# A hybrid attention and expert layer on one core: expert gates written by accumulating indirect DMA instead of one-hot matrix products

## The chip, the cores and the metric

The kernel runs on one core of one Trainium2 chip, written directly against the engines (each engine has its own instruction list and waits on counting semaphores). The metric is device microseconds of that core, lower is better.

## The reference

One decoder layer over 16 meta tokens and 256 sequence tokens, width 2048, float32. Two attention branches and a gated merge come first; the change lies in the last part, the expert mixer:

```python
def peer(h, w_query, sub_keys, expert_u, expert_v):
    ...
    s = jnp.einsum('thcd,hcnd->thcn', q, sub_keys).astype(jnp.float32)
    v1, i1 = lax.top_k(s[:, :, 0], PEER_TOPK)
    v2, i2 = lax.top_k(s[:, :, 1], PEER_TOPK)
    cand = (v1[..., :, None] + v2[..., None, :]).reshape(n_tok, PEER_HEADS, PEER_TOPK * PEER_TOPK)
    best, j = lax.top_k(cand, PEER_TOPK)
    e_idx = (jnp.take_along_axis(i1, j // PEER_TOPK, axis=-1) * PEER_N_KEYS
             + jnp.take_along_axis(i2, j % PEER_TOPK, axis=-1))
    gate = jax.nn.softmax(best, axis=-1)
    ...
        a = jax.nn.gelu(jnp.einsum('cd,chkd->chk', tc, u_sel).astype(jnp.float32), approximate=False)
        w = (gc * a).astype(tc.dtype)
        return jnp.einsum('chk,chkd->cd', w, expert_v[ec])
```

There are 8 heads, each picks 16 of 128 x 128 = 16384 experts for each of the 256 tokens. The kernel computes it densely: gelu(token x every u row), times a gate that is zero except for the picks (summed over heads), times every v row.

## The kernel before, in words

All weights, 376 blocks of 1 MB, pass once through the core in one stream of 752 halves of 512 KB (`load`, L361). The blocks are, in order: 80 for the attention heads (`F_BRANCH` = 80), 16 for the branch outputs, 16 for the output projection, 8 for the query, 128 for u (from block `F_U` = 120), 128 for v (from block `F_V` = 248). The matrices are multiplied as float32 split in two reduced parts, so each half passes three engines:

- SP loads half k into one of four buffers `raw` when the half four places ahead in the stream has been split (`lo_done`).
- ACT copies it to its high part `whi` (`hi_half`, L342), four halves ahead of PE.
- DVE subtracts, `wlo` = `raw` - `whi` (`lo_half`, L349), two halves ahead of PE; `wlo` has two buffers.
- PE multiplies. In `mul_half` (L402, L403, L407) a half takes 24 matmuls of 256 tokens; in `value_block` (L634, L640) it takes 12 of 512 columns.

Each engine's other work is written by hand into slots between the halves.

**u, first 64 blocks** (halves 0 to 127 of the stage). Scores against the sub-keys (L569) are made first. ACT copies them for the first 128 tokens (L817), DVE for the other 128 (L1126), and PE waits for ACT's copy alone before its first u block. ACT then writes gelu of each finished block into `W` (L831). DVE picks: one turn for each of 16 (token tile, head) pairs, spread over the slots of 8 halves (L1143 to L1180).

**Between the two halves of u.** DVE normalises all gates (L1186 to L1190), PE transposes the picked indices and gates (L605), and DVE splits the gates into three bf16 parts (L1197 to L1201).

**u, last 64 blocks.** Beside the stream the dense gates are made, two tokens for each half: DVE builds one-hot rows (`make_rows`, L1213 to L1215), ACT scales two of them (`scale_rows`, L845), PE multiplies them (`gate_pair`, L588, six small matmuls a half) into PSUM, and DVE multiplies the gates of four tokens into `W` over all experts (`apply_gates`, L1234). `W` of these blocks must hold something before, so POOL fills it with ones and gelu comes in by a product (`apply_gelu`, L1240).

```python
            for t in range(2):
                out_ = bank(2 + u // 2 % 2, (2 * (u % 2) + t) * P, P)
                for n in range(3):
                    last = mm(out_, hots[:, u % 2, t, 0, :], hots[:, u % 2, t, 1 + n, :],
                              start=n == 0, stop=n == 2)
```

**v.** `W` of each block is split in a high part (`weight_hi`, L868, ACT) and a low part (`weight_lo`, L1264, DVE), and PE multiplies them by the v rows into all eight PSUM banks. The last token group of the gates has to be applied (L1234) before the first of these.

The buffer `arena` holds `W` (128 x 32768 float32). Its blocks 96 and up also hold what the picks need until they have been used. POOL's only DMAs before are 16 small ones that rearrange rows for the attention (L891).

Of the kernel before, what the change touches and what calls it, by code (L numbers as in the profile page):

```python
# [33 lines left out]
P = 128  # L34
# [27 lines left out]
F_G = F_U + B_U // 2  # L62
# [9 lines left out]
          ("mean128", P), ("swap", P), ("ident", P), ("iota", P), ("iota16", TOPK), ("one", 1), ("rows01", 3)]  # L72
# [13 lines left out]
def shape_constants():  # L86
# [31 lines left out]
    put("iota", np.arange(P)[None, :])  # L118
# [41 lines left out]
def hybrid_layer(nc, stream, x_t, params, consts, h1_rows, out):  # L160
    with ExitStack() as ctx:
# [98 lines left out]
        st = r_work.again().take(4 * HEADS * NK).rearrange("p (i c n) -> p i c n", i=2 * HEADS, c=2)  # L260
# [3 lines left out]
        chosen_i = w4.take(2 * 2 * NSEL).rearrange("p (c s) -> p c s", c=2)  # L264
        chosen_g = w4.take(2 * NSEL)
        gate_sum = w4.take(4 * HEADS)
# [10 lines left out]
        best_all = small[:, 1024:1024 + 2 * NSEL]  # L277
        eq = w4.take(2 * TOPK * TOPK).rearrange("p (c k m) -> p c k m", c=2, k=TOPK)

        part = [small[:, n * P:(n + 1) * P].bitcast(BF16) for n in range(3)]  # L280
        left = [small[:, 512 + n * T:512 + (n + 1) * T] for n in range(2)]

        hots = small[:, 0:1024].bitcast(BF16).rearrange("p (b t n i) -> p b t n i", b=2, t=2, n=4)
        iota_bf = small[:, 1024:1024 + P // 2].bitcast(BF16)
        row2 = small[:, 1088:1088 + 2 * P].bitcast(BF16).rearrange("p (b t i) -> p b t i", b=2, t=2)

        idx_ps = [psum[:, 5 * 512 + n * T:5 * 512 + (n + 1) * T] for n in range(4)]
        gate_sb = [xr[:, 2 * KC * T + n * T:2 * KC * T + (n + 1) * T] for n in range(2)]
# [5 lines left out]
        Whi = [xr[:, n * 2 * T:n * 2 * T + T] for n in range(2)]  # L294
        Wlo = [xr[:, n * 2 * T + T:(n + 1) * 2 * T] for n in range(2)]
# [4 lines left out]
        def f(ap):  # L300
# [23 lines left out]
        sc_ready, sc_taken, best_sub, best_exp, chosen, choice_ps = (  # L324
            sem("head_scores_ready"), sem("head_scores_taken"), sem("best_less_max"), sem("best_exp"), sem("chosen"),
            sem("choice_transposed"))
        const_used, ones_early, ones_late = sem("constants_used"), sem("early_ones_set"), sem("late_ones_set")
        o_ms, o_std_done, heads_normed = sem("head_out_mean_square"), sem("head_out_std"), sem("head_out_normed")
        row_ready, gate_split = sem("one_hot_rows"), sem("gate_parts")
        first_weights = sem("first_weights_done")  # L330
        hot, gate_ps, gated, gelu_done = sem("one_hots"), sem("gates_psum"), sem("gates_applied"), sem("gelu_done")
# [22 lines left out]
        def _(sp):  # L354
# [16 lines left out]
            with sp.Fori(0, BLOCKS // 2 - 1) as i:  # L371
# [18 lines left out]
        def _(pe):  # L390
# [182 lines left out]
            pe.wait_ge(scores_sb, 1)  # L573


            with pe.Fori(0, B_U // 4) as i:
                for q in range(2):
                    mul_block(i * 4 + 2 * F_U, 2 * q, i * 2 + (F_U + q + 1), bank(q, 0, T), hi, lo)


            def gate_pair(i, u):
                pe.wait_ge(hot, i * 4 + (u + 1))
                if u % 2 == 0:
                    pe.wait_ge(gated, i * 2 + (u // 2 + 1))
                for t in range(2):
                    out_ = bank(2 + u // 2 % 2, (2 * (u % 2) + t) * P, P)
                    for n in range(3):
                        last = mm(out_, hots[:, u % 2, t, 0, :], hots[:, u % 2, t, 1 + n, :],  # L588
                                  start=n == 0, stop=n == 2)
                last.then_inc(gate_ps, 1)  # L590

            def late_half(i, m):

                c, j = m // 2, m % 2
                if j == 0:
                    pe.wait_ge(bank_free, i * 2 + (F_G + c + 1))
                mul_half(i * 4 + 2 * F_G, m, bank(c % 2, 0, T), hi[8 * j:8 * j + 8], lo[8 * j:8 * j + 8],
                         j == 0, j == 1)

            late_half(0, 0)  # L600

            pe.wait_ge(chosen, 1)
            for n, src in enumerate((chosen_i[:, 0, :], chosen_i[:, 1, :], chosen_g)):
                for b in range(2):
                    last = nc.tensor.transpose(idx_ps[n][:, b * P:(b + 1) * P], src[:, b * P:(b + 1) * P], C["ident"])  # L605
            last.then_inc(choice_ps, 1)

            late_half(0, 1)
            late_half(0, 2)
            gate_pair(0, 0)  # L610
            late_half(0, 3)
            gate_pair(0, 1)
            gate_pair(0, 2)
            with pe.Fori(0, B_U // 4 - 1) as i:
                for m in range(4, 8):
                    late_half(i, m)
                    gate_pair(i, m - 1)
            gate_pair(0, T // 2 - 1)


            def value_block(base, c, w_base, first):
                pe.wait_ge(w_hi, w_base + c + 1)
                for j in range(2):
# [3 lines left out]
                    if first and j:  # L627
                        pe.wait_ge(gated, T // 4 + 2)
# [16 lines left out]
            pe.wait_ge(bank_free, 2 + F_V)  # L645
# [8 lines left out]
        def _(act):  # L654
# [161 lines left out]
            for c in range(2):  # L816
                last = A(st[:, 0:HEADS, c, :], bank(SCORES[0][c], 0, HEADS * NK).rearrange("p (h n) -> p h n", h=HEADS),  # L817
                         ACT.Copy)
# [4 lines left out]

            act.wait_ge(scores_sb, 1)
            act.wait_ge(scores_dve, 1)
            with act.Fori(0, 2 * HEADS) as i:
                act.wait_ge(sc_taken, i + 1)
                A(sc, st[:, ds(i, 1), :, :].rearrange("p a c n -> p (a c) n"), ACT.Copy).then_inc(sc_ready, 1)
                for q in range(4):
                    act.wait_ge(half_done, i * 8 + (2 * F_U + 2 * q + 2))  # L830
                    A(one_weight(i * 4 + q), bank(q % 2, 0, T), ACT.Gelu).then_inc(bank_free, 1)  # L831
                    for j in range(2):
                        hi_half(act, i * 8 + 2 * F_U, 2 * q + 4 + j)
            A(gate_sum[:, 0:1], C["eps"], ACT.Exp)
            act.wait_ge(best_sub, 1)
            A(chosen_g, chosen_g, ACT.Exp).then_inc(best_exp, 1)


            act.wait_ge(gate_split, 1)

            def scale_rows(i, u):
                act.wait_ge(row_ready, i * 4 + (u + 1))
                for t in range(2):
                    for n in range(2):
                        last = A(hots[:, u % 2, t, 1 + n, :], row2[:, u % 2, t, :], ACT.Copy,  # L845
                                 scale=f(gate_sb[n][:, ds(i * 8 + (2 * u + t), 1)]))
                last.then_inc(hot, 1)

            def act_late_slot(i, m):
                act.wait_ge(half_done, i * 4 + (2 * F_G + m + 1))  # L850
                if m % 2:
                    A(bank(m // 2 % 2, 0, T), bank(m // 2 % 2, 0, T), ACT.Gelu).then_inc(gelu_done, 1)
                hi_half(act, i * 4 + 2 * F_G, m + 4)

            scale_rows(0, 0)
            act_late_slot(0, 0)
            scale_rows(0, 1)
            with act.Fori(0, B_U // 4 - 1) as i:
                for m in range(1, 5):
                    act_late_slot(i, m)  # L860
                    scale_rows(i, m + 1)
            for m in range(B_U - 3, B_U):
                act_late_slot(0, m)
                if m < B_U - 1:
                    scale_rows(0, m + 1)

            def weight_hi(chunk, q):
                A(Whi[q], one_weight(chunk), ACT.Copy).then_inc(w_hi, 1)  # L868


            act.wait_ge(half_done, 2 * F_V)
            act.wait_ge(first_weights, 1)
            act.wait_ge(bank_free, 2 + F_V)
            for q in range(2):
                weight_hi(q, q)
            with act.Fori(0, B_V // 2 - 1) as i:
                for q in range(2):
                    act.wait_ge(half_done, i * 4 + (2 * F_V + 2 * q + 2))
                    act.wait_ge(gated, T // 4 + 2)
# [6 lines left out]
        def _(pool):  # L886

            pool.wait_ge(cum_done, 1)
# [4 lines left out]
            a = r_work.a  # L893
            pool.wait_ge(rows_ps, 3)
            pool.wait_ge(key_scores, 2)
# [11 lines left out]
        def _(dve):  # L907
# [217 lines left out]
            for c in range(2):  # L1125
                last = V.tensor_copy(st[:, HEADS:2 * HEADS, c, :],  # L1126
                                     bank(SCORES[1][c], 0, HEADS * NK).rearrange("p (h n) -> p h n", h=HEADS))
# [220 lines left out]
```

## Time and profile before

| what | before |
|---|---|
| median of three runs | 2360.9 us (2359.17 to 2360.91) |
| the profiled execution: its span, the only time given for it | 2360.5 us |
| PE busy, share of the span | 2309.6 us, 98% |
| DVE busy | 1566.1 us, 66% |
| ACT busy | 1281.2 us, 54% |
| POOL busy | 22.0 us, 1% |
| DMA read | 400.5 MB |

"PE" is the matmul side of TensorE, "PEld" its weight loads, "DMA share" the mean busy share of the 16 DMA engines, "PEclk" the granted TensorE clock as a share of 2.4 GHz. Since successive matmuls overlap, the duration of one is longer than the step from one to the next; the step is read from the chain of waits, which gives each matmul only the time that it adds. An idle time before an instruction is put down to the one that released it.

### The profile page before, as it was taken

The numbers are of one execution on the slowest core, as the hardware profiler recorded it, in microseconds if no ns is written. First come the engines' busy times: TensorE is split into PE (matmuls) and PEld (weight loads), VectorE is DVE, ScalarE is ACT, GpSimd is POOL, SyncE is SP. The second block draws the span as 40 slices with busy tenths as digits, with TensorE's granted clock in tenths as the row PEclk, the third lists the DMA queues.
The fourth block names the chain that finished last, engine by engine and source line by source line (L and its number), as shares of the span: only waits on it lengthen the run. The fifth ranks groups of instructions, "written<-read, shape, count | busy, mean of one in ns | idle before, by whom it ended". The sixth has DMA issues, their size and how long they took to land.

```text
span 2360.5 us, 48307 instructions
## 1 busy us (share of the span) xinstructions
PE 2309.6 (98%) x16398; PEld 2145.8 (91%) x16398; DVE 1566.1 (66%) x2913; ACT 1281.2 (54%) x2068; POOL 22.0 (1%) x25
## 2 busy tenths in 40 slices
PE   6999999999999899999989999999999999999998
PEld 5999999998999899999989999999788888888887
DVE  6666665566664557777779999999555555555555
ACT  5555555555553445555548888888344444444443
POOL 1000000000000010000010000000000000000000
PEclk9999999999999999999999999999999999999999
DMA  4444444444454445555544444444455555555555
GB/s 178 152 151 157 145 154 157 150 151 151 160 178 169 170 160 185 179 177 187 180 143 157 160 160 160 161 163 161 171 195 190 193 195 191 192 195 192 191 194 204
DMA packets 111701, 405.05 MB, mean 172 GB/s; under 512 B 12864, under 2 KB 12992, under 8 KB 111424
## 3 DMA queue, kind: packets, MB, share of 16 engines
q1 hardware_dynamic: 111024, 402.65, 49.7%
q10 hardware_dynamic: 144, 2.10, 0.2%
q8 instruction: 14, 0.23, 0.0%
q0 software_dynamic: 512, 0.02, 0.0%
q14 instruction: 7, 0.06, 0.0%
HBM read 400.50 MB, written 4.19 MB: 171 GB/s over the span
## 4 chain that ended last, share of the span: by engine, by line
PE 96%; DVE 2%; ACT 0%; DMA 0%; issue 0%; DVEq 0%; SPq 0%; ACTq 0%
PE psum L402 20%; PE psum L407 20%; PE psum L403 20%; PE psum L634 20%; PE psum L640 10%; PE psum L588 2%; PE psum L511 0%; PE psum L510 0%; PE psum L479 0%; PE psum L433 0%; PE psum L470 0%; PE psum L478 0%; DVE xr L1201 0%; PE psum L569 0%; DMA arena<-x_t 0%
## 5 line engine op out<-in xcount | busy, mean ns | idle before, releaser
L349 DVE TENSOR_TENSOR wlo<-raw,whi 128x1024 fp32r<-128x1024 f32 x752 | 918.2, 1224 | 652.9 <-PE psum L640 339.2
L402 PE MATMUL psum<-xr,whi 128*128 128x256 f32 (+1 forms) x3968 | 998.4, 289 | 10.4 <-DVE xr L1056 9.0
L403 PE MATMUL psum<-xr,whi 128*128 128x256 f32 (+1 forms) x3968 | 977.9, 283 | 0.0
L342 ACT ACTIVATE whi<-raw 128x1024 fp32r<-128x1024 f32 x752 | 761.5, 1048 | 79.3 <-PE psum L407 63.6
L402 PEld LDWEIGHTS psum<-xr,whi 128*128 128x128 f32 x3968 | 757.5, 191 | 13.0 <-issue 7.4
L403 PEld LDWEIGHTS psum<-xr,whi 128*128 128x128 f32 x3968 | 758.3, 191 | 1.0
L407 PE MATMUL psum<-xr,wlo 128*128 128x256 f32 (+1 forms) x3968 | 559.7, 284 | 8.4 <-DVE wlo L349 8.4
L407 PEld LDWEIGHTS psum<-xr,wlo 128*128 128x128 f32 x3968 | 514.4, 192 | 8.9 <-DVE wlo L349 8.8
L634 PE MATMUL psum<-whi,xr 128*128 128x512 f32 x2048 | 506.8, 390 | 2.6 <-DVE arena L1240 2.6
L634 PEld LDWEIGHTS psum<-whi,xr 128*128 128x128 f32 x2048 | 384.9, 188 | 82.8 <-DVE arena L1240 2.7
L640 PE MATMUL psum<-wlo,xr 128*128 128x512 f32 x1024 | 274.5, 390 | 0.0
L868 ACT ACTIVATE xr<-arena 128x256 fp32r (+1 forms) x128 | 53.6, 419 | 399.2 <-PE psum L640 397.8
L640 PEld LDWEIGHTS psum<-wlo,xr 128*128 128x128 f32 x1024 | 192.8, 188 | 40.1
L845 ACT ACTIVATE small<-small,xr 128x128 bf16<-128x128 bf16 x512 | 163.5, 390 | 85.6 <-DVE small L1215 85.5
L831 ACT ACTIVATE arena<-psum 128x256 f32 x64 | 24.6, 385 | 146.8 <-PE psum L407 146.6
L1234 DVE TENSOR_TENSOR arena<-arena,psum 128x512 f32 (+1 forms) x63 | 85.2, 1353 | 0.0
L1215 DVE TENSOR_SCALAR small<-small,psum 128x128 bf16<-128x128 bf16 x256 | 81.8, 319 | 0.0
L1213 DVE TENSOR_SCALAR small<-small,psum 128x128 bf16<-128x128 bf16 x256 | 65.0, 254 | 3.1 <-PE psum L588 3.0
L588 PE MATMUL psum<-small 128*128 128x128 bf16 x768 | 65.3, 222 | 0.4 <-ACT small L845 0.4
L697 ACT ACTIVATE arena<-psum 128x256 f32<-128x256 f32 (+1 forms) x32 | 12.6, 393 | 96.5 <-PE psum L407 96.5
L1214 DVE TENSOR_SCALAR small<-small,psum 128x128 bf16<-128x128 bf16 x256 | 65.0, 254 | 0.0
L1264 DVE TENSOR_TENSOR xr<-arena,xr 128x256 fp32r<-128x256 f32 x128 | 53.5, 419 | 0.0
(219 smaller groups left out, 1082.6 us busy)
## 6 DMA issues: line engine op xcount, KB each, us to landing
raw<-stream SPq DMA_DIRECT2D x752, 512.0 KB, 3.2
arena<-x_t SPq DMA_DIRECT2D x4, 544.0 KB, 6.5
h_rows<-arena ACTq DMA_DIRECT2D x1, 2048.0 KB, 11.2
raw<-h_rows SPq DMA_DIRECT2D x4, 512.0 KB, 4.4
out<-arena SPq DMA_DIRECT2D x8, 256.0 KB, 3.1
arena<-consts SPq DMA_DIRECT2D x1, 1066.0 KB, 13.2
arena<-params SPq DMA_DIRECT2D x1, 739.0 KB, 10.4
arena<-arena POOLq DMA_DIRECT2D x16, 1.1 KB, 3.2
```

The lines of the kernel that those rows point to most:

```text
L342: nc.scalar.activation(whi[:, s * HALF:(s + 1) * HALF], raw[:, s * HALF:(s + 1) * HALF], ACT.Copy).then_inc(hi_done, 1)
L349: nc.vector.tensor_tensor(wlo[:, k % 2 * HALF:(k % 2 + 1) * HALF], raw[:, s * HALF:(s + 1) * HALF], f(whi[:, s * HALF:(s + 1) * HALF]), AL ...
L402: mm(acc, w, hi[c], start=start and c == 0, stop=False)
L403: mm(acc, w, lo[c], start=False, stop=False)
L407: last = mm(acc, wlo[:, s * HALF + c * P:s * HALF + (c + 1) * P], hi[c], start=False, stop=stop and c == 7)
L588: last = mm(out_, hots[:, u % 2, t, 0, :], hots[:, u % 2, t, 1 + n, :], start=n == 0, stop=n == 2)
L634: mm(bank(b * 4 + j * 2 + n), part[c % 2][:, b * P:(b + 1) * P], whi[:, s * HALF + n * 512:s * HALF + (n + 1) * 512], start=first and part ...
L640: last = mm(bank(b * 4 + j * 2 + n), Whi[c % 2][:, b * P:(b + 1) * P], wlo[:, s2 * HALF + n * 512:s2 * HALF + (n + 1) * 512], start=False, ...
L845: last = A(hots[:, u % 2, t, 1 + n, :], row2[:, u % 2, t, :], ACT.Copy, scale=f(gate_sb[n][:, ds(i * 8 + (2 * u + t), 1)]))
L1213: V.tensor_scalar(hots[:, u % 2, t, 0, :], iota_bf, i1, None, ALU.is_equal)
L1215: last = V.tensor_scalar(hots[:, u % 2, t, 3, :], iota_bf, i2, gate, ALU.is_equal, ALU.mult)
L1234: V.tensor_tensor(w, w, bank(2 + n % 2).rearrange("p (t c) -> p t c", t=4), ALU.mult).then_inc(gated, 1)
```

## The change

The gates are written to a 16.8 MB tensor `gates_at` [128, 128, 256] in device memory (first key, second key, token) and read back one block at a time.

- POOL fills the tensor with zeros in the attention stage: 8 transfers of 2 MB, cut in rows of 512 bytes, one as each head begins.
- DVE finishes each turn of 16 picks inside the turn: address = expert x 256 + token, softmax over the 16. ACT makes the exponentials (L818 of the new file) in the turn too. The turns alternate between the token tiles.
- POOL issues for each of the 16 turns 16 indirect transfers with `compute_op=ALU.add`, each of 128 single float32 values, 256 in all. It waits for the turn's picks, and for the turn two before to have landed.
- PE's u stage is one loop of 128 plain blocks, without one-hot products or transposes. Its accumulators move to banks 2 and 3, so PE waits at its start for DVE's first copy of scores instead of ACT's.
- ACT waits for all scatters before it writes gelu of block 96; SP waits for them before it loads half 488 (8 halves before the end of the u stage).
- SP loads 128 KB of gates for each v block, two ahead, and DVE multiplies them in (`gate_weights`), before both parts of the weight are split off. POOL's fills with ones are gone.

```diff
 @@ SP
+            EARLY = F_V // 2 - 3
+            with sp.Fori(0, EARLY) as i:
...
+            def load_gates(c, n):
+                sp.dma_start(gate_in[n], gates_at[:, ds(c, 1), :].rearrange("p a t -> p (a t)")).then_inc(gates_in[n], 16)
+
+            for b in range(2):
+                sp.wait_ge(scattered[b], 16 * NSEL)
+            for n in range(2):
+                load_gates(n, n)
+            for k in range(4 * EARLY, 2 * F_V):
+                sp.wait_ge(lo_done, k + 1)
+                load(k + 4, k % 4)
+            with sp.Fori(0, B_V // 2 - 1) as i:
+                for q in range(2):
+                    sp.wait_ge(lo_done, i * 4 + (2 * F_V + 2 * q + 1))
+                    load(i * 4 + (2 * F_V + 2 * q + 4), 2 * q)
+                    sp.wait_ge(scaled, i * 2 + (q + 1))
+                    load_gates(i * 2 + (q + 2), q)
+                    sp.wait_ge(lo_done, i * 4 + (2 * F_V + 2 * q + 2))
+                    load(i * 4 + (2 * F_V + 2 * q + 5), 2 * q + 1)
 @@ PE
-            pe.wait_ge(scores_sb, 1)
-            with pe.Fori(0, B_U // 4) as i:
+            pe.wait_ge(scores_dve, 1)
+            with pe.Fori(0, B_U // 2) as i:
                 for q in range(2):
-                    mul_block(i * 4 + 2 * F_U, 2 * q, i * 2 + (F_U + q + 1), bank(q, 0, T), hi, lo)
-            def gate_pair(i, u):
...
+                    mul_block(i * 4 + 2 * F_U, 2 * q, i * 2 + (F_U + q + 1), bank(2 + q, 0, T), hi, lo)
 @@ ACT
+            act.wait_ge(zeroed, 16 * HEADS)
+            with act.Fori(0, HEADS) as i:
+                for b in range(2):
...
+                        if q == 2:
+                            act.wait_ge(best_ready, i * 2 + (b + 1))
+                            A(gate_exp, best, ACT.Exp, bias=neg_best, accum_out=gate_sum[:, 0:1]).then_inc(best_exp, 1)
...
+            expert_blocks(B_U // 2, 3 * B_U // 4)
+            for b in range(2):
+                act.wait_ge(scattered[b], 16 * NSEL)
+            act.wait_ge(rows_out, 16)
+            expert_blocks(3 * B_U // 4, B_U - 4)
 @@ POOL
+            for h in range(HEADS):
+                pool.wait_ge(o_ready, 2 * h + 1)
+                pool.dma_start(blank[:, h * width:(h + 1) * width].rearrange("p (a n) -> p a n", n=P),
+                               spread(zeros.unsqueeze(1), 1, width // P)).then_inc(zeroed, 16)
+            pool.wait_ge(zeroed, 16 * HEADS)
+            every = gates_at.rearrange("p c t -> (p c t)").unsqueeze(1)
+            for h in range(HEADS):
+                for b in range(2):
+                    pool.wait_ge(picked, 2 * h + b + 1)
+                    if h:
+                        pool.wait_ge(scattered[b], 16 * TOPK * h)
+                    for k in range(TOPK):
+                        at = (2 * h + b) * TOPK + k
+                        pool.indirect_dma_start(every, bass.IndirectOffsetOnAxis(pick_at[:, at:at + 1], 0),
+                                                pick_gate[:, at:at + 1], None, compute_op=ALU.add
+                                                ).then_inc(scattered[b], 16)
 @@ DVE
+                        ch.link(V.scalar_tensor_tensor(expert, chosen[:, 0, :], float(NK), chosen[:, 1, :], ALU.mult, ALU.add))
+                        V.tensor_scalar(pick_at[:, mine], expert, float(T), C["token"][:, b:b + 1], ALU.mult, ALU.add)
+                        dve.wait_ge(best_exp, turn + 1)
+                        ch.link(V.reciprocal(gate_sum[:, 1:2], gate_sum[:, 0:1]))
+                        V.tensor_scalar(pick_gate[:, mine], gate_exp, gate_sum[:, 1:2], None, ALU.mult).then_inc(picked, 1)
...
+            def gate_weights(chunk, n):
+                dve.wait_ge(gates_in[n], chunk * 8 + (16 - 8 * n))
+                w = W[:, ds(chunk, 1), :].rearrange("p a t -> p (a t)")
+                V.tensor_tensor(w, w, gate_in[n], ALU.mult).then_inc(scaled, 1)
```

PE, in the loop over the last 64 u blocks, before: the end of one half and the start of the next. `one_hots` is counted by ACT, `gates_applied` by DVE.

```order
L407 MATMUL psum<-xr,wlo 128x256 [waits lo_done]
L407 MATMUL psum<-xr,wlo 128x256 x7
L582 REGISTER_ALU
L584 REGISTER_ALU [waits one_hots]
L588 MATMUL psum<-small 128x128 [waits gates_applied]
L588 MATMUL psum<-small 128x128 x5
L596 REGISTER_ALU
L397 REGISTER_ALU [waits bank_free]
L402 MATMUL psum<-xr,whi 128x256 [waits hi_done]
```

PE at the same place now:

```order
L423 MATMUL psum<-xr,wlo 128x256 [waits lo_done]
L423 MATMUL psum<-xr,wlo 128x256 x7
L429 REGISTER_ALU
L413 REGISTER_ALU [waits bank_free]
L418 MATMUL psum<-xr,whi 128x256 [waits hi_done]
```

The six small matmuls and two waits of each half are gone; what is left is what the first 64 blocks do.

ACT, in a turn of picks now, from the gelu of the third block of the turn to that of the fourth (`head_best_ready` is counted by DVE):

```order
L802 ACTIVATE arena<-psum 128x256
L337 REGISTER_ALU
L338 ACTIVATE whi<-raw 128x1024 [waits half_landed0]
L338 ACTIVATE whi<-raw 128x1024 [waits half_landed1]
L818 ACT_TABLE_LOAD
L818 ACTIVATE arena<-arena 128x16 [waits head_best_ready]
L801 REGISTER_ALU
L802 ISA [waits half_multiplied]
L802 ACT_TABLE_LOAD
L802 ACTIVATE arena<-psum 128x256
```

The exponential brings a table load before it and another before the next gelu, in each of 16 turns.

DVE, in the loop over the v blocks now, one block:

```order
L345 TENSOR_TENSOR wlo<-raw,whi 128x1024 [waits hi_done]
L1178 ISA
L1180 ISA [waits gates_in0]
L1180 TENSOR_TENSOR arena<-arena,small 128x256
L1170 REGISTER_ALU
L344 REGISTER_ALU [waits half_multiplied]
L345 TENSOR_TENSOR wlo<-raw,whi 128x1024 [waits hi_done]
L1183 REGISTER_ALU
L1184 TENSOR_TENSOR xr<-arena,xr 128x256 [waits expert_weight_hi]
```

The product with the gates (L1180) and its wait for SP's transfer stand between the two subtractions of a block.

## Rows read from the trace of the kernel before

**Rows 1.** The page: the chain that ended last, by engine.
```profile
PE 96%; DVE 2%; ACT 0%; DMA 0%; issue 0%; DVEq 0%; SPq 0%; ACTq 0%
```

**Rows 2.** Busy us (x instructions) by stretch; last columns PEclk, DMA share, GB/s.
```profile
core 0: us, PE busy (x) PEld busy (x) DVE busy (x) ACT busy (x) POOL busy (x), PEclk, DMA share, GB/s
36.00:684.00 648.00, 643.81 (x5051) 617.53 (x5050) 404.24 (x555) 359.15 (x603) 7.75 (x16) 0.99 0.45 154
...
854.00:1214.00 360.00, 360.00 (x3002) 360.00 (x3001) 277.17 (x786) 188.54 (x235) 3.73 (x2) 1.00 0.54 181
1245.00:1645.00 400.00, 398.61 (x3663) 393.24 (x3659) 380.74 (x983) 328.07 (x702) 0.00 (x0) 1.00 0.46 159
1663.00:2348.00 685.00, 685.00 (x3024) 567.39 (x3023) 351.22 (x378) 291.85 (x378) 0.00 (x0) 1.00 0.56 193
```

**Rows 3.** The chain: start us, us it adds, what; the u stage's parts.
```profile
850.63 0.31 PE psum L402
...
1215.61 0.96 PE psum L407 x8
1218.49 0.97 PE psum L407 x8
...
1226.92 6.28 DVE xr L1201
...
1650.81 0.97 PE psum L407 x8
...
1655.62 2.95 PE psum L634 x8
1658.56 1.70 PE psum L640 x4
1660.27 1.83 PE psum L634 x8
1662.09 0.91 PE psum L640 x4
```

**Rows 4.** Group of instructions: PE's gate products; busy us, mean ns, idle before.
```profile
L588 PE MATMUL psum<-small 128*128 128x128 bf16 x768 | 65.3, 222 | 0.4 <-ACT small L845 0.4
```

**Rows 5.** Start us, us, DVE between key scores and the first picks.
```profile
850.67 2.35 DVE L1126 COPY arena<-psum 128x1024 f32<-128x1024 f32 x2 [5.72 <-PE psum L569]
```

**Rows 6.** POOL's small transfers (L891), ns min/median/max, and DVE beside them.
```profile
L891 POOL DMA_DIRECT2D arena<-arena x16: 484/484/617, 41.9 to 49.2; - x16
DMA to landing us min/median/max: 1.6/3.2/3.8
...
41.55 2.32 DVE L349 TENSOR_TENSOR wlo<-raw,whi 128x1024 fp32r<-128x1024 f32 x2
44.19 1.23 DVE L349 TENSOR_TENSOR wlo<-raw,whi 128x1024 fp32r<-128x1024 f32 x1 [0.32 <-PE psum L407]
47.20 1.22 DVE L349 TENSOR_TENSOR wlo<-raw,whi 128x1024 fp32r<-128x1024 f32 x1 [1.79 <-PE psum L407]
```

**Rows 7.** DMA queues: packets, MB, share of 16 engines' span.
```profile
q1 hardware_dynamic: 111024, 402.65, 49.7%
q0 software_dynamic: 512, 0.02, 0.0%
```

**Rows 8.** DMA issues: KB each, median us to landing.
```profile
raw<-stream SPq DMA_DIRECT2D x752, 512.0 KB, 3.2
```

**Rows 9.** Groups of DVE and ACT: busy us, mean ns, idle before.
```profile
L349 DVE TENSOR_TENSOR wlo<-raw,whi 128x1024 fp32r<-128x1024 f32 x752 | 918.2, 1224 | 652.9 <-PE psum L640 339.2
L1264 DVE TENSOR_TENSOR xr<-arena,xr 128x256 fp32r<-128x256 f32 x128 | 53.5, 419 | 0.0
L831 ACT ACT_TABLE_LOAD x16 | 20.5, 1283 | 27.7 <-PE psum L407 27.7
```

More of the change, by code:

```diff
@@ L157, in leave, with hybrid_layer @@
         self.base, self.n = self.start + turns * self.per_turn, 0
-def hybrid_layer(nc, stream, x_t, params, consts, h1_rows, out):
+def hybrid_layer(nc, stream, x_t, params, consts, h1_rows, gates_at, out):
     with ExitStack() as ctx:
@@ L276, in hybrid_layer @@
         cand, cand_left = small[:, 512:768], small[:, 768:1024]
-        best_all = small[:, 1024:1024 + 2 * NSEL]
         eq = w4.take(2 * TOPK * TOPK).rearrange("p (c k m) -> p c k m", c=2, k=TOPK)
[L280 to L288, printed above, removed]
+        chosen = w4.take(2 * TOPK).rearrange("p (c m) -> p c m", c=2)
+        expert = w4.take(TOPK)
+        neg_best, gate_exp = w4.take(1), w4.take(TOPK)
+        gate_sum = w4.take(2)
+        gate_in = [small[:, n * T:(n + 1) * T] for n in range(2)]
+        zeros = r_low.again()
+        zeros.take(HEADS * L)
+        zeros = zeros.take(P)
         W = arena[:, :].rearrange("p (c t) -> p c t", c=NK)
@@ L822, in one_weight, with expert_block @@
                 return W[:, ds(chunk, 1), :].rearrange("p a t -> p (a t)")
+            def expert_block(base, i, q):
+                act.wait_ge(half_done, base + 2 * q + 2)
+                A(one_weight(i * 4 + q), bank(2 + q % 2, 0, T), ACT.Gelu).then_inc(bank_free, 1)
             act.wait_ge(scores_sb, 1)
[L825 to L861, printed above, removed]
@@ new lines, in expert_blocks @@
+            def expert_blocks(first, last):
+                with act.Fori(first // 4, last // 4) as i:
+                    for q in range(4):
+                        expert_block(i * 8 + 2 * F_U, i, q)
+                        for j in range(2):
+                            hi_half(act, i * 8 + 2 * F_U, 2 * q + 4 + j)
+            expert_blocks(B_U // 2, 3 * B_U // 4)
+            for b in range(2):
+                act.wait_ge(scattered[b], 16 * NSEL)
+            act.wait_ge(rows_out, 16)
@@ L867, in weight_hi @@
+            expert_blocks(3 * B_U // 4, B_U - 4)
             def weight_hi(chunk, q):
+                act.wait_ge(scaled, chunk + 1)
                 A(Whi[q], one_weight(chunk), ACT.Copy).then_inc(w_hi, 1)
[L871 to L875, printed above, removed]
+            for q in range(4):
+                expert_block(2 * F_V - 8, B_U // 4 - 1, q)
+                if q > 1:
+                    weight_hi(q - 2, q - 2)
+                for j in range(2):
+                    hi_half(act, 2 * F_V - 8, 2 * q + 4 + j)
@@ L1194, in _ @@
-            dve.wait_ge(choice_ps, 1)
-            rest = idx_ps[2]
-            for n in range(3):
-                ch.link(V.tensor_copy(part[n], rest))
-                if n < 2:
-                    ch.link(V.tensor_tensor(left[n], rest, part[n], ALU.subtract))
-                    rest = left[n]
-                last = V.tensor_copy((gate_sb + [idx_ps[3]])[n], part[n])
-                if n < 2:
-                    ch.link(last)
-            last.then_inc(gate_split, 1)
-            dve.wait_ge(gate_split, 1)
@@ new lines, in _, with late_half @@
+            with dve.Fori(0, HEADS) as i:
+                ch.enter(i, 2 * PICK_LINKS)
+                for b in range(2):
+                    pick(i, b)
+                ch.leave(HEADS)
+            def late_half(base, m):
+                dve.wait_ge(half_done, base + (m + 1))
+                lo_half(dve, base, m + 2)
+            with dve.Fori(B_U // 4, B_U // 2 - 2) as i:
+                for m in range(4):
+                    late_half(i * 4 + 2 * F_U, m)
+            def gate_weights(chunk, n):
+                dve.wait_ge(gates_in[n], chunk * 8 + (16 - 8 * n))
+                w = W[:, ds(chunk, 1), :].rearrange("p a t -> p (a t)")
+                V.tensor_tensor(w, w, gate_in[n], ALU.mult).then_inc(scaled, 1)
@@ L1343 @@
     h1_rows = nc.dram_tensor("h1_rows", (P, 2 * D), F32, kind="Internal").ap()
+    gates_at = nc.dram_tensor("gates", (P, NK, T), F32, kind="Internal").ap()
     out = nc.dram_tensor("out", (T, D), F32, kind="ExternalOutput").ap()
[L1345 removed]
+    hybrid_layer(nc, aps["stream"], aps["x_t"], aps["params"], aps["consts"], h1_rows, gates_at, out)
     r = run_bass_kernel_spmd(nc, [arrays], core_ids=[0])
```

205 lines of the change are left out of this document (55 added, 150 removed).

## The prediction

> **What bounds the kernel now.** I read the chain of waits first. 96% of it is PE [rows 1], so time is won only by taking work or waits off PE, and lost only by making PE wait. Next I read the stages. In the first 64 u blocks PE is busy without a gap, in the last 64 for 398.6 of 400 us, in v without a gap, all at the full clock [rows 2]. The other engines have room in the first 64 blocks (DVE 277 of 360 us, ACT 189) and in v (351 and 292 of 685), but hardly in the last 64, where DVE is busy for 381 of 400. POOL does nearly nothing anywhere. Third, the chain around the gates [rows 3]: the first 128 halves of u run from 850.63 to 1219.46 (1218.49 + 0.97), which is 368.8 us or 2.88 us a half. The last 128 end at 1651.78 and the first v product is at 1655.62. So what follows 1219.46 takes 436.2 us until v begins, where 128 plain halves would take 368.8.
>
> **What the change removes.**
> - The gate products and all waits around them. 436.2 - 368.8 = 67.4 us. About 0.38 us of each half is the six products of a pair; they are counted 65.3 us busy [rows 4], but overlap the next half. The remainder is the stall around 1226.92, where DVE splits the gates (6.28 us for one line), and the last group of gates between 1651.78 and 1655.62. The transposes, DVE's splits, the one-hot rows and POOL's fills go too. All of them were beside or in these waits, so they are not counted again.
> - The slow start of v. Its first half takes 2.95 + 1.70 = 4.65 us, its second 1.83 + 0.91 = 2.74 [rows 3]. After the pause PE ran that half at a lower granted clock. Without the pause: 1.9 us.
>
> **What it adds.**
> - A wait at the start of u. PE now needs DVE's first of two copies, which begin at 850.67 and take 2.35 us together [rows 5], where ACT's had long been done. Half of 2.35 and the hand-over: 1.3 us on PE.
> - Between u and v nothing: the weights of block 0 are gated and split in the last halves of u, its first products use banks that u does not, and both gelu and split of the next block take 0.4 us each, for which two halves are there.
> - DVE, first 64 blocks: a turn loses one copy and gains some five operations on 16 columns or fewer, about 1 us in 23, where it idles for (360 - 277)/360 of the time, 5.3 us a turn. The last slot becomes long (over 3 us after the subtraction), but the subtraction now stands ahead of it in that slot, and a part is needed only two thirds into the half after next. Nothing.
> - ACT, first 64 blocks: two table loads of 1.283 us each [rows 9] and an exponential in each turn, 3 us in 23, where it is busy for 52%. It waits for DVE's best values in slot 6, but gelu of a block is needed one block later and `whi` three halves later. Nothing.
> - v: DVE gets 128 products of 128x256, 0.419 us each like its low parts of the weights [rows 9], 54 us beside 685 with 351 busy. SP gets 128 transfers of 128 KB, a fourth of a stream half each [rows 8], one for every two halves: DMA share from 0.56 to about 0.63. A gate transfer goes out nearly 5 us before DVE asks for it, and the stream's, four times its size, land in 3.2. Nothing, as long as it lands in some 8 us: about 3 us more pass before a delay on DVE reaches PE.
> - Zeros, in the attention stage: 32768 rows of 512 bytes. Their cost to the DMA engines is not in the trace. Below: POOL's 512 packets, whose share is given as 0.0%, so under 0.05% of 16 x 2360.5 us, under 37 ns each. Above: 49.7% of 16 x 2360.5 us over 111024 stream packets, 169 ns each [rows 7]. That is 76 to 346 us for each engine in 648 us, of which 45% are used [rows 2]. Even the upper end fits, and each load is asked for some four halves ahead. POOL itself needs 15 ns a row at most (484 ns for a transfer of 32 packets [rows 6]), 62 us for each of 8 transfers, one every 81 us. Nothing.
>
> **The 256 scatters.** This is the unknown on which the sign hangs. Call x the time per transfer at which POOL, or the DMA engines behind it, get through them. The first turn of picks is ready about 879 (851.9 + 8 halves + 4 us), one more follows every 23.05 us, so at x up to 1.44 us POOL keeps pace and the last values land about 1251. ACT must have them before block 96. It has by then made `whi` up to half 195, PE would begin half 196 at 851.9 + 196 x 2.88 = 1416.4, and a gelu and a `whi` come before it: the limit is 1415. With a landing of 3.2 us [rows 6] that gives 879 + 256x + 3.2 = 1415, **x = 2.08 us**. Up to there the scatters cost nothing; beyond it PE stands still for 256 us for each us of x. SP's wait, eight halves before the end, is later and never binds first.
>
> Bounds for x: POOL's transfers took 484 ns each with 32 packets [rows 6, 7]. From below, 0.48 us, if that is all fixed cost. From above, if all of it is by packet: 128 values and 16 counts are 144 packets, 2.18 us; if the addition makes each value count twice, 272 packets, 4.1 us. I take 1.3 us, the middle of 0.48 and 2.18, since a setup for each transfer must be part of the 484 ns. It is a guess in a wide interval, and the limit lies inside it.
>
> **Sum.** -67.4 - 1.9 + 1.3 = -68.0 us on the profiled execution: 2360.5 - 68.0 = 2292.5. The median of the runs lies 0.4 above that execution: 2293.
>
> **Rivals.**
> - *The scatters become the bound (the slower side).* For it: x has 4.1 us as its upper end. Against it: the transfers are small, and POOL is otherwise idle. From x = 2.08 ACT waits ahead of block 96, and behind that wait stand gelu, `whi` and so PE. The gain is gone at 2.08 + 68/256 = 2.35 us. At 3.1 us, the middle of 2.18 and 4.1: 256 x 1.02 = 261 us, so 2554. From 2.35 up I give it 0.22; from 2.08 to 2.35, where a part of the gain is left, 0.07.
> - *POOL stands still while DVE subtracts.* DVE's subtractions take 1.224 of every 2.88 us [rows 9], 42%. If POOL could not work in them, 1.3 us become 2.24: 256 x 0.16 = 41 us, so 2334. Against it: in the 7.75 us of POOL's 16 transfers DVE subtracted for 4.8 us, and the shortest and the median transfer were both 484 ns, the longest 617 [rows 6]. But those read no list of addresses. Chance 0.05. The Trainium skill (SBUF — State Buffer, Who interferes with whom) says that a DVE instruction with two SBUF inputs contends with a GpSimd instruction that reads SBUF; by that rule it is this rival, for the scatters read their addresses there. The rows of the plain transfers show no such thing.
> - *The DMA engines fill up.* 256 x 144 packets at 169 ns are 389 us for each engine, beside 54% of 737 us: 787 us of work in 737, +50, so 2343. At 37 ns they are 85 us and fit. Chance 0.06.
> - *The gates come back late in v.* If their rows of 1 KB take 9 us to land instead of 8, each block waits 1 us: +126, so 2419. Nothing in the rows is that slow under this load. Chance 0.03.
> - *The forecast*, within 2286 to 2304: 0.57.
>
> **The numbers.** About 0.2% (4.7 us) is what a measurement of this kernel can tell from no change. Faster by more: 0.57 + 0.05 + 0.06 and 0.05 of the 0.07 = 0.73. Within it: 0.02, the strip around x = 2.35. Slower: 0.22 + 0.03 = 0.25. The range reaches from 2286 (no wait at the start of u and some stray waits of the attention gone) to 2410, x = 2.53, beyond which about 0.17 is left out. The likeliest case alone has 2286 to 2304.
>
> **What would show it.** PE: all 256 halves of u at 2.88 us, no wait longer than 1.5 us between 852 and the end, v beginning about 1590 at 2.72 us a half and at the full clock. POOL: 256 transfers at 1.0 to 1.44 us, the last before 1260, with pauses between turns. ACT: no wait on the scatters. Wrong would be: POOL's mean above 1.44 us without pauses between the turns, and above 2.08 a wait of ACT and PE near 1416; a DMA share near 1.0 between 880 and 1250 with `whi` waiting for the stream; or DVE waiting for the gate transfers in v.

## The result, and the profile after

| | before | after |
|---|---|---|
| median of 4 runs each, us | 2360.9 (2359.17 to 2361.21) | 2371.89 (2370.98 to 2374.67) |
| span of the profiled execution, us | 2360.5 | 2372.8 |

The ratio is 1.0051, 95% interval 1.0036 to 1.0065: the change makes the kernel 0.5% slower, 11.0 us. 2293 us was forecast. The result lies within the range (2286 to 2410), but on the side that had a chance of 0.25.

The page of the kernel after, its chain by engine and two of its lines of 40 slices (59.3 us each):

```profile
POOL 1000000000000008888888888100000000000000
...
PEclk9999999999999999999999995899999999999999
...
PE 71%; POOL 19%; issue 7%; DVE 2%; ACT 1%; DMA 0%; DVEq 0%; SPq 0%; ACTq 0%; POOLq 0%
```

Where 96% of the chain was PE [rows 1], a fifth is now POOL. That share counts all of POOL's time from 883 us on, while PE worked beside it; what PE lost is read from the waits below. POOL is busy for 8 tenths of ten slices in a row, from 883 to 1490 us, and PE's clock has a hole at the end of that stretch. The waits of the kernel after (engine and line, what was waited for: us, times, longest):

```profile
ACT arena L802 <- issue: 82.2, 1, 82.2
DVE wlo L345 <- ACT whi L338: 78.8, 1, 78.8
...
PE psum L418 <- ACT whi L338: 74.5, 1, 74.5
...
ACT whi L338 <- DMA raw<-stream: 33.8, 33, 2.0
```

One wait of each of three engines, one behind the other. The chain shows their order (start us, us it adds, what):

```profile
1408.73 1.28 POOL gates L877
1410.01 0.94 ACT whi L338
1410.95 81.64 issue
...
1493.41 1.05 ACT whi L338
...
1494.51 0.58 PE psum L418
1495.09 0.21 PE psum L419
...
1499.89 0.12 PE psum L418
...
1669.80 1.84 PE psum L609 x8
1671.64 0.91 PE psum L615 x4
```

ACT stops at 1410.95, at its wait for the scatters ahead of the gelu of block 96, and goes on at 1492.6. The profile names nothing that ended this wait ("issue"); the text finds it in the next view, where the last scatter ends at 1491.08. PE stands still for 74.5 us for want of `whi`. It starts again at the lower of its two clocks (the granted clock from 1494.50 to 1496.00 is 0.50): steps of 0.21 us in place of 0.12, the first half 5.38 us (1494.51 to 1499.89) in place of 2.88. The stop thus costs 74.5 + 2.5 = 77.0 us. What follows is as forecast: v begins with 1.84 + 0.91 us, without the slow first half of before [rows 3].

POOL's scatters in the kernel after (duration ns min/median/max, first and last start us), the waits on them, and their group (busy us, mean ns, idle before them):

```profile
L877 POOL DMA_INDIRECT gates<-arena x256: 1545/2016/2595, 883.5 to 1489.5; - x128
...
  issue: 78.1, 255
...
  ACT arena L802: 82.2, 1
```

The only pauses are the gaps between two scatters, 78.1 us in 255 of them, 0.31 us each: POOL never waits for the next turn. From first start to last end it is 1491.08 - 883.5 = 607.6 us for 256, **2.37 us** a scatter, where I had taken 1.3 and the limit was 2.08. How long a scatter takes depends on where in a subtraction it begins. POOL and DVE of the kernel after in three places, 904 to 910, 1126 to 1133 and 1408 to 1422 (POOL's rows ahead of DVE's; start us, us, engine, line, operation; in brackets the idle time before it):

```profile
906.64 2.04 POOL L877 DMA_INDIRECT gates<-arena  x1 [0.30 <-issue]
...
906.04 1.23 DVE L345 TENSOR_TENSOR wlo<-raw,whi 128x1024 fp32r<-128x1024 f32 x1 [0.22 <-issue]
...
1126.48 2.58 POOL L877 DMA_INDIRECT gates<-arena  x1 [0.30 <-issue]
1129.37 1.54 POOL L877 DMA_INDIRECT gates<-arena  x1 [0.30 <-issue]
...
1126.42 1.22 DVE L345 TENSOR_TENSOR wlo<-raw,whi 128x1024 fp32r<-128x1024 f32 x1 [0.27 <-PE psum L423]
...
1129.37 1.25 DVE L345 TENSOR_TENSOR wlo<-raw,whi 128x1024 fp32r<-128x1024 f32 x1 [0.51 <-PE psum L423]
...
1408.73 2.58 POOL L877 DMA_INDIRECT gates<-arena  x1 [0.30 <-issue]
1411.61 2.57 POOL L877 DMA_INDIRECT gates<-arena  x1 [0.30 <-issue]
...
1417.37 1.54 POOL L877 DMA_INDIRECT gates<-arena  x1 [0.30 <-issue]
...
1408.66 1.23 DVE L345 TENSOR_TENSOR wlo<-raw,whi 128x1024 fp32r<-128x1024 f32 x1 [1.65 <-PE psum L423]
1411.54 1.23 DVE L345 TENSOR_TENSOR wlo<-raw,whi 128x1024 fp32r<-128x1024 f32 x1 [1.65 <-PE psum L423]
```

A scatter that begins just after a subtraction of DVE has begun takes 2.58 us: 1.04 more than 1.54, where 1.16 us of the subtraction are left (from 1408.73 to 1409.89). The one at 906.64 begins in the middle of a subtraction, with 0.63 us of it left, and takes 2.04: 0.50 more. So a scatter is held for what is left of the subtraction less 0.12 us. 169 scatters of the kernel after begin inside a subtraction (0.03 us or more behind its start) with over 0.12 us of it left, and all but the first scatter of the kernel keep to this rule within 0.02 us. One that begins with the subtraction, at 1129.37, takes 1.54, and so do all from 1417, when DVE stands still. So only the scatter's beginning seems to be held. And 2.58 + 0.30 = 2.88 us, the period of a half: once a scatter begins behind a subtraction, the next does too. That is what the steps show. Between 880 and 1225, where picks still shift DVE's subtractions to and fro, 148 scatters come every 2.31 us, 52 of them long. From 1225 to 1418, where DVE has nothing but its subtractions, 69 come every 2.82 us, 63 long. In the stall, with DVE idle, the remaining 39 come every 1.85 us. Altogether 115 of 256 are long (2.5 us or more), 79 take under 1.6 us, and 62 lie between.

POOL's DMA queue in the kernel after (packets, MB, share), and two of its kinds of transfer (KB each, median us to landing):

```profile
q0 software_dynamic: 41600, 16.94, 6.6%
...
gates<-arena POOLq DMA_DIRECT2D x8, 2048.0 KB, 12.5
small<-gates SPq DMA_DIRECT2D x128, 128.0 KB, 3.1
```

POOL's queue had 512 packets before [rows 7]. The zeros add 4224 (e6_zeros_alone, below, has 4736), so the 256 scatters are 41600 - 4736 = 36864, which is 144 each, as forecast. The 32768 rows of zeros had been forecast as one packet each. The DMA engines don't fill up with this (stretches; columns as in [rows 2]):

```profile
884.00:1220.00 336.00, 336.00 (x2803) 336.00 (x2802) 267.56 (x790) 198.22 (x261) 291.40 (x146) 1.00 0.72 183
...
1675.00:2360.00 685.00, 685.00 (x3024) 567.39 (x3023) 393.31 (x503) 291.86 (x378) 0.00 (x0) 1.00 0.65 217
```

PE has no gap in either. The gates of v land in 3.1 us, and nothing waits for them.

### The profile page after: what moved, and what is told of

It reads as the page before. It is cut to its first block, busy times and chain, and to the rows that moved or that the text cites. A ratio compares the mean times of both kernels' runs of the same rounds, so it can differ in the third digit from the quotient of the medians.

```text
span 2372.8 us, 44270 instructions
## 1 busy us (share of the span) xinstructions
PE 2259.3 (95%) x15624; PEld 2102.0 (89%) x15624; DVE 1367.0 (58%) x2195; ACT 1109.4 (47%) x1570; POOL 551.4 (23%) x285
## 3 DMA queue, kind: packets, MB, share of 16 engines
q0 software_dynamic: 41600, 16.94, 6.6%
## 4 chain that ended last, share of the span: by engine, by line
PE 71%; POOL 19%; issue 7%; DVE 2%; ACT 1%; DMA 0%; DVEq 0%; SPq 0%; ACTq 0%; POOLq 0%
PE psum L609 20%; POOL gates L877 19%; PE psum L423 13%; PE psum L418 12%; PE psum L419 12%; PE psum L615 10%; PE psum L527 0%; PE psum L526 0%; PE psum L495 0%; PE psum L486 0%; PE psum L449 0%; PE psum L494 0%; PE psum L585 0%; DMA arena<-x_t 0%; PE psum L549 0%
## 5 line engine op out<-in xcount | busy, mean ns | idle before, releaser
L345 DVE TENSOR_TENSOR wlo<-raw,whi 128x1024 fp32r<-128x1024 f32 x752 | 920.4, 1225 | 881.7 <-PE psum L423 505.0
L418 PE MATMUL psum<-xr,whi 128*128 128x256 f32 (+1 forms) x3968 | 991.7, 287 | 85.4 <-ACT whi L338 74.5
L877 POOL DMA_INDIRECT gates<-arena x256 | 529.5, 2068 | 440.8 <-DVE arena L1161 362.6
L802 ACT ACTIVATE arena<-psum 128x256 f32 (+1 forms) x128 | 49.3, 385 | 414.7 <-PE psum L423 332.3
L865 POOL DMA_DIRECT2D gates<-arena x8 | 13.6, 1698 | 457.4 <-ACT arena L719 457.4
L1180 DVE TENSOR_TENSOR arena<-arena,small 128x256 f32 (+1 forms) x128 | 53.6, 419 | 0.0
L679 ACT ACTIVATE arena<-psum,arena 128x256 f32 x32 | 15.2, 475 | 69.9 <-PE psum L423 69.5
L966 DVE RECIPROCAL arena<-arena 128x528 f32<-128x528 f32 x8 | 27.6, 3448 | 0.0
## 6 DMA issues: line engine op xcount, KB each, us to landing
gates<-arena POOLq DMA_DIRECT2D x8, 2048.0 KB, 12.5
```

The source lines that it names most:

```text
L345: nc.vector.tensor_tensor(wlo[:, k % 2 * HALF:(k % 2 + 1) * HALF], raw[:, s * HALF:(s + 1) * HALF], f(whi[:, s * HALF:(s + 1) * HALF]), AL ...
L418: mm(acc, w, hi[c], start=start and c == 0, stop=False)
L802: A(one_weight(i * 4 + q), bank(2 + q % 2, 0, T), ACT.Gelu).then_inc(bank_free, 1)
L877: pool.indirect_dma_start(every, bass.IndirectOffsetOnAxis(pick_at[:, at:at + 1], 0), pick_gate[:, at:at + 1], None, compute_op=ALU.add).t ...
L1180: V.tensor_tensor(w, w, gate_in[n], ALU.mult).then_inc(scaled, 1)
```

## The experiments

**Theory, after the result.** A scatter alone costs POOL 1.54 + 0.30 us. If it begins while DVE subtracts with both inputs in SBUF, it is held for the rest of the subtraction; it locks in phase with the halves, and so comes to 2.37 us. ACT's wait at block 96 hands that on to PE. Rivals: the DMA engines or the addition in device memory hold POOL; PE loses time elsewhere too.

### e1_moved: what is the change worth without ACT's wait

The wait protects the scatters' addresses and values, which lie in the place of `W`'s blocks 96 and 97, where gelu of these blocks would overwrite them. They are moved to columns of `xr` that are free until SP has seen the scatters, and ACT waits only until the picks are made.

```diff
-        pick_at = w4.take(2 * NSEL).bitcast(U32)
-        pick_gate = w4.take(2 * NSEL)
+        pick_at = xr[:, 2 * KC * T:2 * KC * T + 2 * NSEL].bitcast(U32)
+        pick_gate = xr[:, 2 * KC * T + 2 * NSEL:2 * KC * T + 4 * NSEL].bitcast(F32)
...
-            for b in range(2):
-                act.wait_ge(scattered[b], 16 * NSEL)
+            act.wait_ge(picked, 2 * HEADS)
```

> The addresses and gates of the picks move from the place of W's blocks 96 and 97 to 512 columns of xr that nothing uses until the end of the u stage; ACT waits only for the picks, not for the scatters, before block 96. If the 78 us between the changed kernel (2371.9) and my forecast are the wait for the scatters alone: no wait of ACT near 1411, PE's u stage is 256 halves of 2.88 us, v begins at about 1591, 2294 us in all, while POOL still takes about 2.4 us for each transfer. A rival: the scatters slow the stream itself, or v pays for the gate transfers; then u is longer than 738 us or v longer than 697 us, and the time stays above 2300.

Measured: 2295.58 us (2294.58 to 2297.11, 5 runs), ratio to before 0.9727 (0.9713 to 0.974). That is 76.3 us less than the kernel after, and the stop had been read as 77.0. The scatters are no faster:

```profile
L876 POOL DMA_INDIRECT gates<-xr x256: 1545/2574/2595, 881.5 to 1527.7; - x128
```

The last begins at 1527.7, 38 us later than before the edit, since PE and DVE don't stop any more and none come at 1.85 us: 154 of 256 are long. Nobody waits for them. So all of the loss is this one wait, and nearly all of the gain forecast (68 us) is there beside it. The start of u differs from the forecast in one thing (the chain of this kernel; one row of 0.21 stands for 14):

```profile
850.30 1.24 DVE arena L1100
851.54 0.32 issue
851.86 0.38 PE psum L418
...
852.38 0.21 PE psum L418
...
855.36 1.11 PE psum L423 x8
```

The wait for DVE's copy is 1.24 us (1.3 forecast), but half a microsecond behind it PE's steps go from 0.12 to 0.21 us, and its first half takes 4.61 us (851.86 to 856.47, mean granted clock 0.63), not 2.88. Those 1.7 us were not in the sum. It is the slow start that I had taken off at v and not put on here.

### e2_moved_banks: the start of u

Beside e1's edit, the key scores' banks are exchanged, so that PE waits for ACT's copies and not DVE's.

```diff
-        SCORES = ((6, 0), (2, 4))
+        SCORES = ((2, 6), (0, 4))
...
-            pe.wait_ge(scores_dve, 1)
+            pe.wait_ge(scores_sb, 1)
```

> e1, and the score banks swapped, so that PE's first u block waits for ACT's copy of scores, which is done before, instead of for DVE's. If that wait costs what the trace of the changed kernel shows (1.26 us), 1.3 us less than e1: 2292.7. If PE's start there hangs on something else, no difference.

Measured: 2292.83 us (2292.22 to 2293.31, 5 runs), ratio to before 0.9714 (0.97 to 0.9727): 2.75 us less than e1, more than twice the wait of 1.24. The key scores end at 850.80, the chain has no wait behind them, and v begins at 1588.26 (1590.87 in e1):

```profile
850.80 0.31 PE psum L418
```

The wait (1.24 + 0.32) and the slow half behind it (1.7) go together. This kernel beats both, by 2.9% and 3.3%.

### e3_one_sbuf_input: what holds POOL

The subtraction in u takes its second operand from PSUM and is otherwise the same in size and duration.

```diff
+            nc.vector.tensor_tensor(wlo[:, k % 2 * HALF:(k % 2 + 1) * HALF], raw[:, s * HALF:(s + 1) * HALF],
+                                    bank(0, 0, HALF), ALU.subtract).then_inc(lo_done, 1)
...
-                    lo_half(dve, base, m + 2)
+                    lo_half_u(dve, base, m + 2)
```

> The changed kernel, but in the u stage DVE's subtraction takes its second operand from PSUM (old scores) instead of whi: the low parts of u are wrong and so is the output; the length of the instruction stays near 1.2 us. If POOL's transfers are held up by the two-input subtractions (shared port), x falls from 2.38 to about 1.85 us, nearly all transfers at 1.54 to 1.7 us, the last at about 1360, no wait of ACT, 2294 us. If x is POOL's or the DMA engines' own time, x stays at 2.3 to 2.4 and the time at 2372.

Measured: 2295.7 us (2293.42 to 2296.47, 4 runs), ratio 0.9725 (0.971 to 0.974), with ACT's wait in its place. The scatters by their line:

```profile
L884 POOL DMA_INDIRECT gates<-arena x256: 1544/1546/1818, 881.1 to 1356.1; - x128
```

The group of the subtraction:

```profile
L353 DVE TENSOR_TENSOR wlo<-raw,psum 128x1024 fp32r<-128x1024 f32 x248 | 302.6, 1220 | 262.0 <-PE psum L430 259.5 <-issue 2.5
```

A scatter that begins 0.52 us into a subtraction, and that subtraction:

```profile
1239.82 1.55 POOL L884 DMA_INDIRECT gates<-arena  x1 [0.30 <-issue]
...
1239.30 1.22 DVE L353 TENSOR_TENSOR wlo<-raw,psum 128x1024 fp32r<-128x1024 f32 x1 [1.66 <-PE psum L430]
```

By the rule of the kernel after it would have taken 1.54 + 0.70 - 0.12 = 2.12 us. None of 256 takes 2.5 us or more; 249 take under 1.6. All 256 last from 881.1 to 1357.7, 1.86 us each. DVE's instruction is as long as before (1220 ns to 1225) and just as frequent. The one thing taken away is its second input in SBUF, and with it the hold, the wait and 76.2 us. This settles the cause on DVE's side. Which of the scatter's own steps is held, no run isolates. The Trainium skill (SBUF — State Buffer, Who interferes with whom) says that a DVE instruction with two SBUF inputs contends with a GpSimd instruction that reads SBUF, and that one with at most one SBUF input, outside the 2-port performance modes, does not. The two runs agree in both halves, 2.58 against 1.54 us. The lock for a whole instruction, by whichever engine starts first, that this page of the Trainium skill (section SBUF: two separate sides) states as well, does not show in the other direction: of 61 subtractions that began while a scatter ran, none took over 1.26 us, like the one that began with a scatter at 1129.37 (1.25). None of the 61 began between 0.1 and 0.7 us into a scatter, so that part is not shown.

### e4_half_scatters: half the number

```diff
-                    for k in range(TOPK):
+                    for k in range(0, TOPK, 2):
```

(and the counts of the three waits halved)

> The changed kernel with 128 of the 256 transfers (every second pick is left out, so half of the gates are missing). By the law end = 883.5 + n x, with limit 1415: eight transfers a turn take at most 8 x 2.88 = 23 us, so POOL keeps pace with the picks, the last lands before 1260, no wait, 2294 us. If instead another cost of the change (gates in v, table loads, the zeros) holds the time, it stays above 2300.

Measured: 2296.01 us (2295.41 to 2297.25, 4 runs), ratio 0.9729 (0.9714 to 0.9744).

```profile
L877 POOL DMA_INDIRECT gates<-arena x128: 1543/2269/2592, 881.3 to 1245.3; - x128
```

POOL now keeps pace with the turns (128 scatters over 364 us), while 58 of 128 are as long as ever. So it is the number of scatters times their length against a limit, and a scatter that is held costs nothing below it. All three kernels without ACT's long wait, e1, e3 and e4, agree within 0.5 us.

### e7_wait_at_88: the law beyond the limit

ACT's wait is put 8 blocks, 46.1 us, earlier.

```diff
-            expert_blocks(B_U // 2, 3 * B_U // 4)
+            expert_blocks(B_U // 2, 3 * B_U // 4 - 8)
...
-            expert_blocks(3 * B_U // 4, B_U - 4)
+            expert_blocks(3 * B_U // 4 - 8, B_U - 4)
```

> The changed kernel, with ACT's wait for the scatters before block 88 instead of 96, 46.1 us earlier. If POOL is slow because DVE subtracts, it speeds up to 1.85 us as soon as PE, and with it DVE, stands still: 16 more transfers are left then, and the stall grows by 16 x 1.85 = 30 us, to 2401. If a transfer takes 2.38 us whatever DVE does, the stall grows by the whole 46 us, to 2418.

Measured: 2400.45 us (one run, so without an interval). PE's stop in it, and the scatters:

```profile
PE psum L418 <- ACT whi L338: 104.1, 1, 104.1
```

```profile
L877 POOL DMA_INDIRECT gates<-arena x256: 1545/1725/2593, 880.2 to 1469.8; - x128
```

The stop grows by 29.6 us, not by 46.1, since once DVE has stopped too, what is left goes at 1.85 and not at 2.88 us a scatter. The stall speeds up what it waits for. The last scatter begins at 1469.8, not at 1489.5. PE's first half behind the stop takes 5.12 us (1474.81 to 1479.93). The law is 256x up to the point where DVE stops, and a flatter one behind it.

### e6_zeros_alone: the zeros

The kernel before, with the 8 zero transfers and ACT's wait for them.

```diff
+            for h in range(HEADS):
+                pool.wait_ge(o_ready, 2 * h + 1)
+                pool.dma_start(blank[:, h * width:(h + 1) * width].rearrange("p (a n) -> p a n", n=P),
+                               spread(zeros.unsqueeze(1), 1, width // P)).then_inc(zeroed, 16)
```

> The kernel before, with the eight transfers of zeros in the attention stage and nothing else of the change. If they cost nothing, 2360.5 us as before (in the trace of the changed kernel PE reaches 681.6 us at the same point as before it). If their 33 waits of ACT for the stream reach PE, up to 30 us more.

Measured: 2360.73 us (2359.63 to 2362.05, 10 runs) beside 2361.27, ratio 1.0 (0.999 to 1.0009). They cost nothing, as forecast.

### e5_no_add and e8_moved_no_add: plain writes in place of additions

```diff
-                                                pick_gate[:, at:at + 1], None, compute_op=ALU.add
+                                                pick_gate[:, at:at + 1], None
```

e5 is the kernel after with this edit, e8 is e1 with it.

> The changed kernel with plain indirect writes in place of the adding ones (where two heads pick the same expert for a token one gate is lost). If the addition is part of what POOL has to do for each value, its transfers get shorter than 1.54 us and x falls below 2.38 us; if the length is the 128 addresses and the start of a transfer alone, 1.54 and 2.58 us stay, and 2372 us.

> e1 with plain indirect writes instead of adding ones (where two heads pick the same expert for a token one gate is lost). In e5 PE stood still for 0.2 to 1.8 us between single matmuls that wait for nothing, all through the time of the scatters, and the u stage became about 150 us longer. If plain indirect writes do that, it happens here too: u is far longer than 738 us and the time is near 2295 + 150 = 2445. If it was that one run, POOL keeps pace at 1.26 us, the last transfer is at about 1245, and the time is 2295.

Measured: e5 2445.17 us (one run); e8 2397.92 us (2387.76 to 2413.74, 3 runs), ratio 1.0162 (1.0094 to 1.0231). For e5 no theory had this; e8 was run to see whether it needs ACT's wait for the scatters, and came out between its two cases. The addition does cost POOL something: the scatters of e5 take 0.96 us alone, not 1.54 (the hold is there too: 72 of the 74 that begin inside a subtraction take 0.96 us and what is left of it less 0.12), and there are (12928 - 4736)/256 = 32 packets to one, not 144. The queue of e5:

```profile
q0 software_dynamic: 12928, 16.94, 2.8%
```

Its scatters by their line:

```profile
L877 POOL DMA_INDIRECT gates<-arena x256: 956/962/1967, 883.4 to 1385.4; - x128
```

But PE itself gets slower while they run. The stretch 884 to 1220 of e5:

```profile
884.00:1220.00 336.00, 286.78 (x1977) 272.23 (x1976) 187.52 (x559) 139.62 (x184) 184.20 (x165) 0.85 0.40 129
```

One of its waits and a piece of its chain:

```profile
PE psum L418 <- issue: 26.8, 43, 1.8
```

```profile
1005.31 0.37 PE psum L418
1005.68 1.80 issue
1007.48 0.37 PE psum L419
1007.85 1.03 issue
```

The same stretch of e8:

```profile
884.00:1220.00 336.00, 298.80 (x2211) 286.98 (x2210) 208.83 (x620) 156.67 (x206) 214.81 (x183) 0.90 0.46 144
```

In 336 us e5's PE gets 1977 matmuls done where the kernel after has 2803. Between single matmuls there are gaps of up to 1.8 us in which PE waits for no semaphore, and its clock falls to 0.85. It isn't a full DMA: the engines' share is 0.40 where it was 0.72. That e8 has it too, where ACT waits for no scatter, shows that it belongs to the plain writes. Its size varies from run to run by 26 us in e8. What holds PE's instructions back was not found.

## Why the prediction was wrong

- **Step that failed: the size of x.** "I take 1.3 us, the middle of 0.48 and 2.18, since a setup for each transfer must be part of the 484 ns." With it the scatters stood in the sum at nothing. It measured 2.37 us: 1.54 for the scatter, 0.31 for the gap behind it, and 0.52 of standing still on the average. The two ends had been taken from plain transfers [rows 6] and counted packets alone. POOL's own 1.85 us lies near the upper end (2.18) and under the limit: with it alone the forecast would have held, as e3 shows.
- **The rival that was right and got 0.05.** "POOL stands still while DVE subtracts" was worked out as 42% of all time lost, 1.3 us to 2.24. Two faults, which pull apart: its base was too small, and it took the loss as a share of time, by which 1.85 us would have become about 3.2 (an estimate, 1.85/0.58). In the trace a scatter is held once at most, for what is left of a subtraction, and 2.58 + 0.30 being a half's period sets each scatter just behind the start of the next subtraction. "Against it" stood that plain transfers were not held. They weren't, but as the same text said, they read no list of addresses. That this is the difference that counts is likely and not shown. The rule of the Trainium skill (SBUF — State Buffer, Who interferes with whom), which spoke for the rival, held for the scatters, and e3 shows it.
- **The law was right in form.** 879 + 256x + 3.2 against 1415 gives for 2.37 an overrun of 74 us, and 2293 + 256 x 0.29 = 2367 beside 2371.89 measured; the break-even was put at 2.35. But its x is no constant: e1, where DVE never stops, needs 2.53 us a scatter (881.5 to 1530.3), which by the law would be an overrun of 115 us. The 74 come out because the 2.37 were measured with the 39 fast scatters of the stall in them, and e7 shows that these depend on where the stall begins. With x so near it, the sign hung on hundredths of a microsecond, and the strip around it deserved more than 0.02.
- **ACT's and PE's limit.** PE stopped at 1420.0 (1494.51 - 74.5), where 1416.4 was forecast. The 3.6 us are the later start of u in this execution, 853.83 for 851.9, and the slow half behind its wait, 1.7. Landing took 1.5 us (1491.08 to 1492.6), not 3.2.
- **The products of the gates, the stall at 1226.92, the last group.** Gone as forecast: e1 has all 256 halves at 2.88 us but the first, and v begins at 1590.87.
- **Start of u.** 1.24 us for 1.3, but with 0.32 and a slow half of 1.7 us more. That is most of the 2.6 us by which e1 lies above 2293.
- **v.** 2.72 us a half at the full clock, DVE 393 us busy where 351 + 54 was forecast, DMA share 0.65 for 0.63. Nothing waits for the gates. Rival with 0.03 rightly low.
- **DMA engines full.** Share 0.72 from 884 to 1220, where the rival needed 1. A packet of POOL's queue took 60 ns on the average (6.6% of 16 x 2372.8 us over 41600), nearer to the 37 than to the 169. ACT waits for the stream 33 times, 33.8 us in all, without a gap on PE. The zeros keep POOL for 1.7 us each, where the upper bound was 62, and land in 12.5.

## What to carry to other kernels

Price a new instruction on an idle engine by what it reads and what its neighbours read at that moment, not by its nearest relative: here a stream of small indirect transfers took 28% longer (2.37 for 1.85 us each) because most of them (162 of 256) began inside a DVE subtraction with two SBUF inputs and were held by it, and one input in PSUM undid it. When a slack engine has a deadline, look at what the deadline protects; moving 2 x 256 columns of addresses and values was worth 76 us. And in these runs a wait of PE cost its length plus a slow restart: 1.7 us after a wait of 1.2, 2.5 after one of 74.5 and 2.2 after one of 104.1 (e7).

## What the runs showed of the hardware

- An indirect transfer of 128 single float32 values costs POOL 1.54 us with an addition (144 packets) and 0.96 without (32 packets), and 0.30 between two.
- When it begins inside a DVE subtraction with two SBUF inputs, it takes longer by what is left of the subtraction less 0.12 us, from 1.54 up to 2.58 us (168 of 169 in the kernel after within 0.02 us). With the subtraction's second input in PSUM, 249 of 256 take under 1.6 us.
- Plain indirect writes of single values slow PE down (1977 matmuls in 336 us for 2803), where accumulating ones do not; the cause stays open.
- A transfer that writes 2 MB in 4096 rows of 512 bytes occupies POOL for 1.70 us, three and a half times a small one of 484 ns [rows 6], and makes 528 packets, not 4096.
